# Latent attention by pairs of heads: one product for the rotated queries of a pair, rotated scores on two row halves, one PSUM bank for projections

## The reference, cut to what matters

```python
z = h @ w_in
cq = rms_norm(z[..., :Q_LORA], q_norm)
ckv = rms_norm(z[..., Q_LORA:Q_LORA + KV_LORA], kv_norm)
k_pe = apply_rope(z[..., Q_LORA + KV_LORA:], cos, sin)
q = (cq @ w_qb).reshape(B, L, MLA_HEADS, QK_NOPE + QK_ROPE)
q_pe = apply_rope(q[..., QK_NOPE:], cos[:, :, None, :], sin[:, :, None, :])
kv = (ckv @ w_kvb).reshape(B, L, MLA_HEADS, QK_NOPE + V_DIM)
# for each block of 128 queries:
s = (einsum('bqhd,bkhd->bhqk', qn, k_nope) + einsum('bqhr,bkr->bhqk', qp, k_pe)) * scale
p = softmax(where(causal, s, -1e30))
o = einsum('bhqk,bkhd->bqhd', p, v)
```

## Time and profile before

| | |
|---|---|
| median of 3 runs | 2726.39 us (2726.22 to 2728.03) |
| the profiled execution | 2724.2 us |
| its span | 2722.5 us, 1.7 us of the time lie around it |
| mean granted TensorE clock | 0.939 |
| TensorE busy | 2475.7 us, 91% |
| VectorE busy | 1757.0 us, 65% |
| ScalarE busy | 1138.3 us, 42% |
| latent stage | 1476.3 to 1515.1 us |
| latent attention stage | 1515.1 to 1642.7 us |

### The profile page before, as it was taken

One profiled execution on the slowest core, in us unless ns is written; L12 is line 12 of the kernel. 1 busy time (PEld: TensorE's weight loads), 2 busy tenths in 40 slices (PEclk: granted clock), 3 DMA queues, 4 the chain that ended last, 5 costly groups with the idle time before them and its releaser, 6 DMA issues. The chain is left out here.

```text
span 2722.5 us, 32575 instructions
## 1 busy us (share of the span) xinstructions
PE 2475.7 (91%) x12679; PEld 1956.2 (72%) x12679; DVE 1757.0 (65%) x2552; ACT 1138.3 (42%) x1635; POOL 45.4 (2%) x153
## 2 busy tenths in 40 slices
PE   7999799999999998699994898999997989899998
PEld 6666587677767876588872456788886877688886
DVE  6899645487775666799965565677766473742434
ACT  4444332154554224588853343622324144441323
POOL 0000001000000000100001000000000000000000
PEclk8999799999999986799996999999998889999998
DMA  6787636232324643899963113134332414233321
GB/s 240 266 282 250 240 95 264 79 100 83 101 81 174 250 94 139 320 398 419 417 244 135 55 46 101 62 112 148 111 109 87 111 37 151 64 107 93 96 90 32
DMA packets 299642, 427.90 MB, mean 157 GB/s; under 512 B 27706, under 2 KB 213549, under 8 KB 289632
## 3 DMA queue, kind: packets, MB, share of 16 engines
q1 hardware_dynamic: 291648, 395.92, 42.7%
q0 software_dynamic: 5392, 20.97, 1.9%
q10 hardware_dynamic: 2448, 8.91, 0.8%
HBM read 384.63 MB, written 41.14 MB: 156 GB/s over the span
## 5 line engine op out<-in xcount | busy, mean ns | idle before, releaser
L3619 PE MATMUL banks<-big,late_parts 128*128 128x512 f32 x1920 | 443.4, 393 | 11.1 <-DVE late_parts L3792 7.3
L3619 PEld LDWEIGHTS banks<-big,late_parts 128*128 128x128 f32 x1920 | 363.7, 190 | 89.3 <-DVE late_parts L3792 7.5
L3619 PE MATMUL banks<-h_parts_second,late_parts 128*128 128x512 f32 x1440 | 332.6, 392 | 12.8 <-DVE h_parts_second L3816 12.8
L3619 PEld LDWEIGHTS banks<-h_parts_second,late_parts 128*128 128x128 f32 x1440 | 272.1, 189 | 70.9 <-issue 14.4
L3792 DVE TENSOR_TENSOR late_parts<-w_second,late_parts 128x2048 fp32r<-128x2048 f32 x69 | 158.0, 2291 | 218.8 <-ACT late_parts L3681 218.7
L2322 DVE TENSOR_TENSOR expert_parts<-w,expert_parts 128x2048 fp32r<-128x2048 f32 x102 | 233.0, 2289 | 29.0 <-ACT expert_parts L2318 28.6
L3681 ACT ACTIVATE late_parts<-w_second 128x2048 fp32r<-128x2048 f32 x69 | 132.0, 1914 | 256.1 <-PE banks L3619 256.1
L1309 PE MATMUL banks<-h_parts,ssm_parts 128*128 128x512 f32 x960 | 232.9, 400 | 4.9 <-DVE ssm_parts L1577 4.4
L2318 ACT ACTIVATE expert_parts<-w 128x2048 fp32r<-128x2048 f32 x102 | 194.7, 1916 | 63.9 <-PE banks L2329 63.9
L1309 PEld LDWEIGHTS banks<-h_parts,ssm_parts 128*128 128x128 f32 x960 | 180.6, 191 | 51.2 <-issue 9.4
L2329 PE MATMUL banks<-expert_parts,expert_xt 128*128 128x512 f32 x816 | 195.0, 399 | 5.7 <-DVE expert_xt L2846 5.7
(11 more groups left out here) (690 smaller groups left out, 3744.8 us busy)
## 6 DMA issues: line engine op xcount, KB each, us to landing
w_second<-in_mlp_w_dram SPq DMA_DIRECT2D x64, 1024.0 KB, 5.2
w<-in_w_exp_gate_dram SPq DMA_DIRECT2D x34, 1024.0 KB, 7.8
w<-in_w_exp_up_dram SPq DMA_DIRECT2D x34, 1024.0 KB, 7.4
w<-in_w_exp_down_dram SPq DMA_DIRECT2D x34, 1024.0 KB, 8.9
w<-in_w_in_dram SPq DMA_DIRECT2D x64, 512.0 KB, 4.6
w<-in_mod_mix_w_dram SPq DMA_DIRECT2D x24, 1024.0 KB, 5.1
w<-in_mod_ffn_w_dram SPq DMA_DIRECT2D x24, 1024.0 KB, 5.1
w<-in_w_in_dram SPq DMA_DIRECT2D x16, 1024.0 KB, 6.9
```

The costliest lines, as they stand in the source:

```text
L3619: mm = pe.matmul(ps[:, bank(n, f), :], w_part(n, w)[:, kk, f * P:(f + 1) * P], x[:, v, kk, :], start=(first_chunk(n) and kk == 0 and j == ...
```

## The change

Heads are taken in pairs; a step u is one pair and one block of queries, 16 steps with two units each.

- `LatentWeights` replaces `LatentHeads`. It holds four slots of unrotated query weights and of key-value weights, and for each pair one matrix `w_rope` of 128 columns, the rotated query weights of both heads side by side. The weights of pair 0 are loaded in the latent stage, of pair 1 when the attention stage begins, of pair j from 2 on when the values of pair j - 2 are made.
- cos, sin and k_pe have 128 rows; the latent stage copies rows 0 to 63 to rows 64 to 127 (two copies in its middle, one at its end).
- `rope_queries` makes both heads' rotated queries in one product of 128 output rows; `rotated` rotates them in one go with four swaps of 32 rows and three passes over 128 rows.
- `logits(u)` makes the unrotated scores of both heads in banks u * 2 % 4 and the next, then both rotated ones, from rows 0 to 63 and 64 to 127.
- All projections but those of pair 0 use bank 7 (`PROJ`), rotated queries included. Queries, keys and values of the next pair stand at the first three steps of a pair, one head's ahead of the turn and the other's behind it; the rotated queries of the pair after next at the fourth.
- `weigh(u)` follows `turn(u)` in the same step and uses bank 6, half of it for each head; a hand-over takes two blocks of both heads, every other step.
- The scale is negative, and `row_max` is one fused operation with a 512-wide mask, which VectorE makes when the stage begins. Probabilities, turned blocks, the mask and a scratch tile lie in k.h.

```diff
@@ latent_stage @@
-def latent_stage(k, loads, cq, ckv, k_pe, cos, sin):
+def latent_stage(k, loads, weights, cq, ckv, both_k_pe, both_cos, both_sin):
+    k_pe, cos, sin = (t[0:ROPE, :] for t in (both_k_pe, both_cos, both_sin))
...
             sp.dma_start(pos_i[:], k.ins["positions_2"]).then_inc(s["pos_loaded"], 16)
+            weights.load(sp, 0)
...
             step(dve.tensor_scalar(sin[0:half, :], sin[0:half, :], -1.0, None, ALU.mult))
+            step(dve.tensor_copy(both_cos[ROPE:, :], cos))
+            step(dve.tensor_copy(both_sin[ROPE:, :], sin))
...
                                                   op0=ALU.mult, op1=ALU.mult))
+            step(dve.tensor_copy(both_k_pe[ROPE:, :], k_pe))
...
+class LatentWeights:
+
+
+    def __init__(self, k, sb):
+        self.k, self.nq = k, QL // P
+        self.loaded = [k.stack.enter_context(k.nc.semaphore(f"latent_w_loaded{n}")) for n in range(2)]
+        self.wq, self.wkv = sb("wq", [P, 4, self.nq, NOPE]), sb("wkv", [P, 4, NOPE + VD])
+        self.w_rope = sb("w_rope", [P, 2, self.nq, 2 * ROPE])
+
+    def load(self, sp, j):
+        ins = self.k.ins
+        for i in (2 * j, 2 * j + 1):
+            first, at = i * (NOPE + ROPE), i % 2 * ROPE
+            sp.dma_start(self.w_rope[:, j % 2, :, at:at + ROPE], columns(ins["mla_w_qb_2"][0], first + NOPE, ROPE)).then_inc(self.loaded[j % 2], 16)
+            sp.dma_start(self.wq[:, i % 4], columns(ins["mla_w_qb_2"][0], first, NOPE)).then_inc(self.loaded[j % 2], 16)
+            sp.dma_start(self.wkv[:, i % 4], ins["mla_w_kvb_2"][0][:, i * (NOPE + VD):(i + 1) * (NOPE + VD)]).then_inc(self.loaded[j % 2], 16)
...
+        WEIGH, PROJ = 6, 7
+        FIRST = {"qn0": 4, "qn1": 5, "kn0": 6, "kn1": 3, "v0": 2, "v1": 1}
+
+        def bank(j, name):
+            return FIRST[name] if j == 0 else PROJ
...
+            weights.load(sp, 1)
+            for j in range(pairs):
+                if j >= 2:
+                    sp.wait_ge(s["v_done"], 2 * (j - 1))
+                    weights.load(sp, j)
+                first_half(k, sp, j, ahead)
...
+            def rope_queries(j):
+                pe.wait_ge(weights.loaded[j % 2], 96 * (j // 2 + 1))
+                if j == 1:
+                    pe.wait_ge(s["rotated"], 1)
+                elif j:
+                    pe.wait_ge(s["v_copied"], 2 * j)
+                for c in range(nq):
+                    mm = pe.matmul(ps[:, PROJ, :], weights.w_rope[:, j % 2, c, :], cq[:, c, :], start=(c == 0), stop=(c == nq - 1))
                 mm.then_inc(s["qp_done"], 1)
+            def query(j, hh):
+                if j and hh == 0:
+                    pe.wait_ge(s["rotated"], j + 1)
+                elif j:
+                    pe.wait_ge(s["qn_copied"], 2 * j + 1)
...
+            def logits(u):
+                j, n = u // TB, (u % TB + 1) * P
+                if u % TB == 0:
+                    pe.wait_ge(s["qn_copied"], 2 * j + 2)
+                    pe.wait_ge(s["kn_copied"], 2 * j + 2)
+                    pe.wait_ge(s["rotated"], j + 1)
...
+                for hh in range(2):
+                    unit = 2 * u + hh
+                    if unit >= 4:
+                        pe.wait_ge(s["exp_done"], unit - 3)
+                    pe.matmul(ps[:, unit % 4, 0:n], qn[:, j % 2, hh, n - P:n], kn[:, j % 2, hh, 0:n], start=True, stop=False)
+                for hh in range(2):
+                    unit, rows = 2 * u + hh, slice(hh * ROPE, (hh + 1) * ROPE)
+                    pe.matmul(ps[:, unit % 4, 0:n], qp[rows, j % 2, n - P:n], k_pe[rows, 0:n], start=False, stop=True).then_inc(s["scores_done"], 1)
+
+            def weigh(u):
+                j, b = u // TB, u % TB
+                pe.wait_ge(s["turned_copied"], 2 * u + 2)
+                if b == 0:
+                    pe.wait_ge(s["v_copied"], 2 * j + 2)
+                if b % 2 == 0 and u:
+                    pe.wait_ge(s["o_low"], u // 2)
+                for hh in range(2):
+                    at = hh * HALF + b % 2 * P
+                    for kb in range(b + 1):
+                        mm = pe.matmul(ps[:, WEIGH, at:at + P], v[:, j % 2, hh, kb, :], pt_tiles[:, hh, kb * P:(kb + 1) * P], start=(kb == 0),
+                                       stop=(kb == b))
                 mm.then_inc(s["weighed"], 1)
+            rope_queries(0)
+            for hh in range(2):
+                query(0, hh)
+            for hh in range(2):
+                key(0, hh)
+            for hh in range(2):
+                value(0, hh)
+            rope_queries(1)
             logits(0)
+            for u in range(TB * pairs):
+                j, b = u // TB, u % TB
+                further = j + 1 < pairs
+                if u + 1 < TB * pairs:
+                    logits(u + 1)
+                if further and b < 3:
+                    (query, key, value)[b](j + 1, 0)
+                turn(u)
+                if further and b < 3:
+                    (query, key, value)[b](j + 1, 1)
+                if j + 2 < pairs and b == 3:
+                    rope_queries(j + 2)
+                weigh(u)
...
+            exponents(0)
+            for u in range(TB * pairs):
+                j, b = u // TB, u % TB
+                further = j + 1 < pairs and b < 3
+                if further:
+                    (copy_query, copy_key, copy_value)[b](j + 1, 0)
+                if u + 1 < TB * pairs:
+                    exponents(u + 1)
+                copy_turned(u)
+                if further:
+                    (copy_query, copy_key, copy_value)[b](j + 1, 1)
...
+            def rotated(j):
+                dve.wait_ge(s["qp_done"], j + 1)
+                if j >= 2:
+                    dve.wait_ge(s["scores_done"], UNITS * (j - 1))
+                src = ps[:, PROJ, :]
+                for first in range(0, P, ROPE):
+                    for at, other in ((first, first + half), (first + half, first)):
+                        ins = dve.tensor_scalar(swapped[at:at + half, :], src[other:other + half], scale, None, ALU.mult)
+                        ins.then_inc(s["rope_step"], 1)
+                step.n += 4
+                step(dve.scalar_tensor_tensor(out=raw[:], in0=src, scalar=scale, in1=cos[:], op0=ALU.mult, op1=ALU.mult))
+                step(dve.tensor_tensor(swapped[:], swapped[:], sin[:], ALU.mult))
+                dve.tensor_tensor(qp[:, j % 2], raw[:], swapped[:], ALU.add).then_inc(s["rotated"], 1)
+                dve.wait_ge(s["rotated"], j + 1)
...
+                    dve.tensor_tensor_reduce(out=ps[:, unit % 4, 0:n], in0=ps[:, unit % 4, 0:n], in1=wide_mask[:, T - n:T], scale=1.0,
+                                             scalar=3e38, op0=ALU.add, op1=ALU.min, accum_out=nmax[:, unit:unit + 1]).then_inc(s["max_done"], 1)
...
+            dve.memset(wide_mask[:, 0:T - P], 0.0).then_inc(s["mask_ready"], 1)
+            dve.tensor_scalar(wide_mask[:, T - P:], k.future_mask[:], -1.0, None, ALU.mult).then_inc(s["mask_ready"], 1)
             rotated(0)
+            dve.wait_ge(s["mask_ready"], 2)
+            rotated(1)
             row_max(0)
+            for u in range(TB * pairs):
+                j, b = u // TB, u % TB
+                if u + 1 < TB * pairs:
+                    row_max(u + 1)
+                normalise(u)
+                if u and b % 2 == 0:
+                    hand_over(u // 2 - 1)
+                if b == 3 and j + 2 < pairs:
+                    rotated(j + 2)
+            hand_over(2 * pairs - 1)
```

279 lines of the change are left out of this document (98 added, 181 removed).

## The result

The change makes the kernel slower by about a third of a per cent: 2736.42 us (2729.84 to 2743.95, 20 runs) against 2727.11 (2718.85 to 2732.74, 20 runs), ratio 1.0034 [1.0026, 1.0042], so +9.3 us [7.1, 11.4]. The forecast was 2728.6 in a range of 2720 to 2736.5, so the median lies in it by 0.08 us. As a difference to the kernel before, +9.3 was measured where +2.2 was forecast, and that is beyond the 5.5 us that the prediction had set as the bound of no change. The profiled execution has a span of 2737.1 us at a mean granted clock of 0.934; before it was 2722.5 at 0.939.

A forecast was written before the change was run, and what follows sets the result against it. The stage was taken as bound by TensorE's work in its steady part; new waits eat the gain per pair, leaving -2.2 us, and 4.4 for the clock makes +2.2: 2728.6 us, range 2720 to 2736.5.

The forecast's parts named there:

- Start: Head of the latent attention: early weights start TensorE at 1515.9 against 1519.06; first scores 1528.2; slow clock there costs 1.7 us.
- Side by side: Rotated scores of two heads on two row halves cost as one head's; a pair's scores 7.64 us, against 11.16.
- Rival D: Row halves do not run side by side in banks holding unrotated scores: 2738 us, chance 0.06.
- Waits in the steady pair: TensorE waits for the rotation, before turns and before weighings: 5.7 us per pair, eating the gain per pair.
- Rival B: Faster, as waits in pairs 0 to 2 fall away: 2715 us if half, 2707 if all; chance 0.15.
- Work in a pair: TensorE's work for one pair, priced by start-to-start times: 23.5 us against 29.1 for two heads before.
- The clock: Granted clock falls beside waits, two stretches in pair 3 and half a chance in pair 0: 4.4 us, bounds 0 to 11.5.
- Sum: Whole stage: hand-over ends at 1640.5, 2.2 us sooner at full clock; with 4.4 for the clock, +2.2; chance 0.42.
- the signs that I had named: Right if turn waits are 0.9 to 1.4 us, pairs 29 us, first record near 1516; wrong if pairs exceed 31 us.
- Rival C: Slower: clock falls in pair 3 before the third scores and stays low to the end: 2735.7 us, chance 0.15.
- rival A: Clock stays high, since falls are tied to idle gaps longer than any here: -2.2 us, 2724.2; chance 0.22.

The follow-up runs named there:

- filled_all_pairs: The change plus throwaway products before the last pair's first three turns and before the first query product of pairs 0 to 2: 2726.27 us, ratio 0.9997 to before.
- best_scores_by_head: all_first_and_rope_in_head with scores made head by head, so the two row halves never run side by side: 2719.09 us, ratio 0.9975 to before.
- fill_last_pair: The change plus throwaway 512-column products ahead of the turns of the last pair's first three steps (one, two, two): 2729.11 us, ratio 1.0017 to before.
- all_first_and_rope_in_head: scale_and_copy_first plus rotated queries ahead of the turn, pair 1's ahead of pair 0's values, and weighings waiting per head: 2704.37 us, ratio 0.9914 to before.
- copy_first_only: The change with ScalarE copying turned weights of step u before the exponentials of u+1, VectorE's order kept: 2730.76 us, ratio 1.0011 to before.
- scale_first_only: The change with VectorE scaling step u and handing over before the maxima of u+1, ScalarE's order kept: 2726.48 us, ratio 0.9993 to before.
- scale_and_copy_first: The change with both lists reordered: VectorE scales u before maxima of u+1, ScalarE copies u before exponentials of u+1: 2712.30 us, ratio 0.9953 to before.

## Why the prediction came out as it did

Taking 2.63 off the times of after and setting them beside the sum:

- **Start.** First product at 1516.06 (1515.9), first scores at 1528.21 (1528.2). The 64-row copy took 0.42 (0.5). Right in time. I had the clock fall in the gap; it is at 1.00 up to 1519.5 in the profile's own time, 0.8 us into the first product, and at 0.50 from 1520 to 1523. The rotated and the unrotated query products there take 1.8 us more for it (2.66 for 1.88, and 4.63 for the 3.60 of filled_all_pairs), where I had 1.7.
- **Side by side.** Two heads' 512-wide rotated scores take 1.13 in the banks that already hold the unrotated ones, and the pair's scores are 7.65 (7.64). Rival D is out, and best_scores_by_head puts the gain at 3.7 us per pair. Right, from a row of another stage.
- **Waits in the steady pair.** In pair 2, 6.0 us against 6.45: before the query product 1.83 (1.5) and 0.47 (0.45), before the turns 0.58, 0.88, 1.24 (0.90, 1.22, 1.38). The waits that were said to eat the gain do. Rival B, that they fall away, is out. In pair 0 the wait was 2.65 (2.3).
- **Work in a pair.** Pair 2 has 23.4 us beside its waits, where I had 21.75: pair stretches were 33.25, 31.78, 29.39 (30.9, 29.2, 28.2). I priced each product by its start-to-start time. A product that the next one waits behind costs its whole duration: of the key products one takes 1.12 and not 0.87. The six projections are 1.2 of the 1.65 us (the two value products take 1.16 and 1.19 for 0.89 each), and turns, weighings and scores up to 0.1 each. The difference is 1.0 in the kernel where hardly any wait is left (24.5 of 25.95, with 23.5 in the sum).
- **The clock: the step that failed in size.** I took 4.4 us for it, "two such stretches in pair 3 and a half chance of one" in pair 0 (two and a half times 1.7 are 4.25). It fell in pair 0 (query product 3.17 for 1.98, and the turn behind it 0.64 for 0.38), pair 1 (3.67 for 1.98), and in the last pair from near 1629 to 1642.7. There the 384-wide scores took 4.35 us to their end, for 2.30 in pair 2, the 512-wide ones 4.15 for 2.94, and the two weighings and the turn between them 1.8 more (1.19, 2.08 and 1.12 for 0.68, 1.16 and 0.70, as fill_last_pair and pair 2 have them): 5.1. With 1.5 and 1.7 that is 8.3. The step that was mis-sized is the number of stretches: pair 1 had none in my sum, and the last pair cost three of 1.7 us and not two. Filling the waits takes 6.5 us off the stage, with the products' own time still in it.
- **Sum.** From the last pair's 256-wide scores to VectorE's end are 29.56 us where the sum had 24.0 (22.5 and the hand-over). The misses are +2.35, +2.6, +1.2 and +5.6 = 11.7, less the 4.4 allowed for: 7.3 us, which is +2.2 made into +9.5. About 3.9 of it is clock (8.3 less 4.4), 3.4 the work and the longer rotation waits.

Of the signs that I had named, most came: scalings ended the waits before the turns, records of 64 rows stand side by side, the first record is near 1516. But two of the three steady waits before turns (0.58, 0.88) lie under the 0.9 that I had given, and one sign of being wrong came too: pairs 0 and 1 took over 31 us (33.25 and 31.78). That the median still lies in the range is luck: it does by 0.08 us, where single runs of the change spread over 14.

Rival C was the nearest in size (2735.7) and in its place: the clock did fall before the third scores of the last pair. But it came back within the last ones, and not at the end. My reading of the earlier trace rows was incomplete: TensorE idles no longer than 1.2 us up to the fall near 290, but in the low stretch behind it there are waits of 2.61, 1.87 and 1.71 us, and in that the place is not the same. Between the stage's first and last product no gap exceeds 2.65 us, and the clock fell three times, each time in a wait or within 1 us behind it. The Trainium skill (TensorE: Matmul & The Clock Gate, section HAM oscillation), which I used for rival A, ties the fall to long gaps. The trace does not agree with that as the only case. The Trainium skill (TensorE: Matmul & The Clock Gate, section A second HAM failure mode: psum-queue depth-cycling) tells of a kernel whose clock goes up and down over short idles between groups of products. The trace agrees with that one, which I had left out: in all_first_and_rope_in_head, where no gap behind the first product exceeds 0.78 us, the clock is 1.00 from 1527 us to the last product.

What was not in any of my cases is that the waits come from the order on VectorE and ScalarE, and not from the pairs. I had named that order and priced the chain that it makes, but took it as given and did not ask what order would open it. That is worth 0.47% against before with the two lists alone, 0.86% with the edits of all_first_and_rope_in_head.

## What to carry to other kernels

In a pipeline in which each engine does step u+1 and step u, whatever releases another engine for step u goes first, on every engine of the chain at once: one engine alone took 4.6 or 1.1 us of TensorE's idle time away, both together 13.7. Where a bound engine gets waits of 1 to 2 us, count the clock: here it cost 8.3 us, more than the 6.0 of waits in a pair, and work with no use in those waits took back the whole slowdown by the runs. Price work with a wait behind it by its duration, not by the distance to the next start.

## What the runs showed of the hardware

The clock does not follow the length of a wait. With the same 1.83 us wait before the query product, copy_first_only has it low in pairs 1 and 2, scale_first_only in neither:

```profile
1563.00:1566.00 3.00, 2.88 (x6) 0.94 (x4) 2.12 (x8) 0.51 (x2) 0.00 (x0) 0.54 0.00 0
...
1593.00:1596.00 3.00, 2.87 (x5) 1.12 (x6) 2.78 (x11) 0.00 (x0) 0.00 (x0) 0.66 0.00 0
```

(windows of copy_first_only; in scale_first_only the rows of that product read 1.98 us both times, here 3.03 and 3.01). Nor does one kernel do the same in each pair: behind that wait the change has 3.67 in pair 1 and 1.98 in pair 2, scale_and_copy_first 1.98 and then 3.46. Such a term can only be given as a range.

The rotated scores of two heads on two row halves cost what those of one head cost, 1.13 us for four 512-wide records against 1.12 for two. A step that goes from 128 to 64 rows and back twice instead of once takes 1.56 us for 0.96 at 128 columns and 4.12 for 2.87 at 512. How much of that is the second change of rows and how much the lost overlap, no run here separates.
